# The first expert block's rows picked by TensorE inside the router phase, and block 1 of the second stage turned inside block 0's products

## The chip, the cores and the metric

The kernel runs on one core of one Trainium2 chip, as one launch. It computes two transformer blocks one after the other on 512 tokens of width 1024, all in float32. The metric is the device time of one execution in microseconds (us). Each core has a matrix engine (TensorE, PE below), a vector engine (DVE), a scalar engine (ACT), GpSimd (POOL) and SyncE (SP), which here only issues DMAs. Matrix products land in eight PSUM banks of 128 x 512 float32 words.

## The reference, cut to what matters

Both blocks end in a mixture of experts (MoE). Block 1 has 32 experts of width 256 and picks 2 of them per token; block 2 has 32 experts of width 1024 and picks 4. The second block's MoE is the same in outline, with a bias, a clamp and another gate.

```python
h2 = modulate(rms_norm(x, norm_ffn[l]), shift2, scale2)
ffn = hierarchical_moe(h2, ...)

def hierarchical_moe(h, w_group, b_group, w_router, b_router, w_gate, w_up, w_down):
    t = h.reshape(-1, d)                       # 512 x 1024
    ...                                        # softmax over groups, then top 2 of the experts of one group
    combine = ...                              # 512 x 32, two weights per token
    for e in range(N_EXPERTS):
        hid = jax.nn.silu(t @ w_gate[e]) * (t @ w_up[e])
        out = out + combine[:, e:e + 1] * (hid @ w_down[e])
```

The kernel computes for each expert only the tokens that chose it.

## The kernel before, in words

`two_blocks` calls a chain of phases. Each phase is a set of instruction streams, one per engine, and ends in a barrier of all engines. The change touches two phases, and each runs twice (names with rt1 and ex1 for the first MoE, rt2 and ex2 for the second; "first stage" and "second stage" below).

**The router phase** (`router_phase`, lines 1642 to 1872). The activations stand in `xT`, features on partitions. PE turns them (`turn_rows(n)`, line 1700: four 128x128 transposes each, n from 0 to 7, two per 128 tokens), ACT scales them by each token's inverse norm into `htok(i)` (line 1740; tokens 0 to 255 into the two slots of `x_rows`, the rest into `rt_late`) and stores them to DRAM as `rows` (line 1743). Meanwhile DVE picks the experts of each token; `asg` is the 0-1 matrix of tokens by experts. PE counts the tokens of each expert (lines 1708, 1710), ranks each token inside its expert (`lt` and `pre`, lines 1712 and 1717), and spreads a table of constants to all partitions (`beats`, `chosen`, lines 1715 and 1719). From these DVE works out (lines 1817 to 1841) the slot of each token in a list of rows. Then comes "the map": DVE and POOL make 0-1 matrices (`hot`, `put`) and PE multiplies them (line 1729), which turns "token to slot" into "slot to token". DVE and ACT write it out as `index` and `table` (lines 1859 to 1866). Between, PE runs products with no use (`keep_warm`, line 371). SP waits until the stores of `rows` have landed; then the phase ends.

**The expert phase** (`expert_phase`, lines 1886 to 2515). The experts are worked off in a fixed order of blocks, each with parts N (64 rows), Q (32 rows) or W (128 rows). In the first stage block 0 is one N part of 64 rows. In the second stage it is N and Q, 96 rows in all. For a block: POOL gathers its rows from `rows` by an indirect DMA with `index` (line 1880; `gather`), PE turns them (`transpose_x`, line 2112; eight tiles' worth, one call is `x_block`), ACT and in part DVE copy them from PSUM to `ex_xt` with the norm's gain and the modulation's shift (`copy_x`, lines 2266 and 2440), PE multiplies by the expert's up weights (`up_products`, line 2138), DVE and ACT apply the gate, PE turns the result (line 2156) and multiplies by the down weights (line 2179), DVE copies it out (line 2421) and ACT stores it.

PE works in this order: x_block(0), up(0), x_block(1), up(1), x_block(2), then the a and down steps of block 0, and so on. `ahead(b)` says for which blocks x_block(b + 1) is put between the products of up(b): before, only for some later blocks of the first stage.

The weights come in pieces of 1 MB. An expert's up weights are 2 pieces in the first stage and 8 in the second, its down weights 1 and 4. Sixteen places ("seats") hold them: `ring`, `x_spare` and `hT`. The first sixteen pieces are loaded before or during the router phase. Every later piece is issued by SP when PE has done the last product with the piece that sat there (line 2053, semaphore `used`). So the stream of weights starts again only when PE uses the first piece of block 0. `turns` (line 1955) loads a loop count from `table` into a register of each engine, at the start of the phase.

```python
x_block(0)
up_block(0)
x_block(1)
up_block(1)
```

## Time and profile before

| | us |
|---|---|
| median of 3 runs | 2619.21 |
| lowest, highest | 2614.50, 2623.94 |
| the profiled execution | 2614.59 |
| its span in the trace | 2612.8 |
| PE busy | 2383.2 (91%) |
| DVE busy | 1054.8 (40%) |
| ACT busy | 587.6 (22%) |
| POOL busy | 259.1 (10%) |
| HBM read | 640.14 MB |

All rows come from the profiled execution. Its own time lies 0.1 us above the lowest run and 4.6 us under the median. Times in the rows are microseconds from the start of the span. A row of the timeline is a run of equal instructions: start, length, engine, line, output and input, shapes, count, and in brackets how long the engine had stood idle before and what released it. A float32 product is two passes of PE, so that it counts twice in the trace; a transpose is one pass.
### The profile page before, as it was taken

The numbers are of one execution on the slowest core, as the hardware profiler recorded it, in microseconds if no ns is written. First come the engines' busy times: TensorE is split into PE (matmuls) and PEld (weight loads), VectorE is DVE, ScalarE is ACT, GpSimd is POOL, SyncE is SP. The second block draws the span as 40 slices with busy tenths as digits, with TensorE's granted clock in tenths as the row PEclk, the third lists the DMA queues.
The fourth block names the chain that finished last, engine by engine and source line by source line (L and its number), as shares of the span: only waits on it lengthen the run. The fifth ranks groups of instructions, "written<-read, shape, count | busy, mean of one in ns | idle before, by whom it ended". The sixth has DMA issues, their size and how long they took to land. (4 is left out here: it accounts for less than half of the span.)

```text
span 2612.8 us, 34138 instructions
## 1 busy us (share of the span) xinstructions
PE 2383.2 (91%) x12722; PEld 1153.3 (44%) x12722; DVE 1054.8 (40%) x2414; ACT 587.6 (22%) x1536; POOL 259.1 (10%) x272
## 2 busy tenths in 40 slices
PE   7999888989876999999999988999899998999984
PEld 3444666555344555667444442333233342333323
DVE  4856665743223655468332142232222322122215
ACT  3223532023222311364110011111111111111213
POOL 0000002111111000077200010000000000000002
PEclk8999978989988999899999989999999999999996
DMA  8533503979998310010314148999999999999995
GB/s 338 221 145 123 184 1 119 392 268 417 399 372 311 117 36 0 33 65 34 133 65 163 64 176 312 419 417 417 419 414 386 417 419 419 419 418 418 419 415 181
DMA packets 144204, 684.85 MB, mean 262 GB/s; under 512 B 16456, under 2 KB 44248, under 8 KB 78488
## 3 DMA queue, kind: packets, MB, share of 16 engines
q1 hardware_dynamic: 120920, 635.19, 60.3%
q0 software_dynamic: 9376, 25.19, 2.6%
q10 hardware_dynamic: 13744, 22.30, 2.3%
q8 instruction: 102, 1.67, 0.3%
q14 instruction: 62, 0.51, 0.1%
HBM read 640.14 MB, written 49.02 MB: 264 GB/s over the span
## 5 line engine op out<-in xcount | busy, mean ns | idle before, releaser
L2138 PE MATMUL bank<-ring,ex_xt 128*64 128x512 f32 (+4 forms) x2240 | 360.1, 507 | 24.4 <-DMA ring<-in_up 19.0
L2266 ACT ACTIVATE ex_xt<-bank,mod,gain 128x64 f32<-128x64 f32 (+2 forms) x472 | 151.0, 416 | 736.1 <-PE bank L2112 729.0
L2138 PE MATMUL bank<-x_spare,ex_xt 128*64 128x512 f32 (+4 forms) x1504 | 274.2, 522 | 23.5 <-DMA x_spare<-in_up 18.8
L2138 PEld LDWEIGHTS bank<-ring,ex_xt 128*64 128x64 f32 (+2 forms) x2240 | 125.3, 130 | 240.1 <-issue 194.3
L2179 PE MATMUL bank<-ring,ex_at 128*32 128x256 f32 (+2 forms) x1168 | 193.2, 502 | 13.8 <-DMA ring<-in_down 9.1
L1880 POOL DMA_INDIRECT x_rows<-rows,index x74 | 75.5, 1020 | 1078.5 <-PE bank L2112 1058.3
L2138 PEld LDWEIGHTS bank<-x_spare,ex_xt 128*64 128x64 f32 (+2 forms) x1504 | 98.1, 137 | 184.5 <-issue 147.0
L2179 PE MATMUL bank<-x_spare,ex_at 128*64 128x512 f32 (+2 forms) x720 | 133.8, 516 | 13.0 <-DMA x_spare<-in_down 12.1
L2680 PE MATMUL bank<-hT,ring 128*128 128x512 f32 x320 | 140.8, 594 | 2.5 <-ACT hT L2730 2.5
L2421 DVE COPY ex_y<-bank 128x512 f32<-128x512 f32 (+1 forms) x83 | 48.1, 599 | 214.6 <-PE bank L2179 214.5
L2179 PEld LDWEIGHTS bank<-ring,ex_at 128*32 128x32 f32 (+2 forms) x1168 | 61.1, 127 | 129.3 <-issue 109.0
L2378 DVE TENSOR_TENSOR ex_hb<-bank,ex_bias 128x512 f32<-128x512 f32 x40 | 27.5, 687 | 223.2 <-PE bank L2138 223.2
L1566 PE MATMUL bank<-u_mix,ring 128*128 128x512 f32 x256 | 114.2, 603 | 1.8 <-PEq L319 1.8
L2378 DVE TENSOR_TENSOR ex_hb<-bank,cst 128x512 f32<-128x512 f32 x40 | 27.5, 687 | 212.8 <-PE bank L2138 212.6
L633 PE MATMUL bank<-hT,ring 128*128 128x512 f32 x256 | 113.4, 597 | 0.0
L2680 PEld LDWEIGHTS bank<-hT,ring 128*128 128x128 f32 x320 | 60.4, 190 | 72.0 <-issue 70.2
L2179 PEld LDWEIGHTS bank<-x_spare,ex_at 128*64 128x64 f32 (+2 forms) x720 | 46.3, 134 | 89.3 <-issue 68.8
L3154 PE MATMUL bank<-hT,ring 128*128 128x512 f32 x192 | 83.8, 593 | 0.0
L2138 PE MATMUL bank<-hT,ex_xt 128*64 128x512 f32 (+4 forms) x400 | 78.6, 548 | 4.6 <-DMA hT<-in_up 4.6
L2278 ACT ACTIVATE ex_at<-bank 128x512 f32<-128x512 f32 (+2 forms) x62 | 28.4, 483 | 234.9 <-PE bank L2156 234.9
L633 PEld LDWEIGHTS bank<-hT,ring 128*128 128x128 f32 x256 | 48.0, 191 | 61.3 <-issue 61.0
L1566 PEld LDWEIGHTS bank<-u_mix,ring 128*128 128x128 f32 x256 | 48.4, 192 | 60.3 <-issue 60.2
(583 smaller groups left out, 3336.3 us busy)
## 6 DMA issues: line engine op xcount, KB each, us to landing
ring<-in_up SPq DMA_DIRECT2D x170, 1024.0 KB, 23.3
x_spare<-in_up SPq DMA_DIRECT2D x120, 1024.0 KB, 26.0
ring<-in_down SPq DMA_DIRECT2D x82, 1024.0 KB, 26.7
x_spare<-in_down SPq DMA_DIRECT2D x64, 1024.0 KB, 22.1
hT<-in_up SPq DMA_DIRECT2D x30, 1024.0 KB, 19.0
ring<-in_w_in SPq DMA_DIRECT2D x14, 2048.0 KB, 12.8
ring<-in_w_ada SPq DMA_DIRECT2D x12, 2048.0 KB, 8.4
ring<-in_w_mod SPq DMA_DIRECT2D x12, 2048.0 KB, 8.8
```

Of the source, the lines that this page charges most:

```text
L633: last = nc.tensor.matmul(o[:, :], w[:, kk, c0:c0 + P], k.hT[:, kk, :], **f)
L1566: last = nc.tensor.matmul(k.ps[m][:, :], w[:, kk, m * P:(m + 1) * P], mix[:, h * KT + kk, :], start=h == 0 and kk == 0, stop=h == halves - ...
L1880: pool.indirect_dma_start(out=to(p)[:, 0:D // groups], out_offset=None, in_=k.a["rows"].rearrange("r (g d) -> (r g) d", g=groups), in_offs ...
L2138: last = nc.tensor.matmul(k.ps[up_bank(b, p, r)][g * rows:(g + 1) * rows, 0:c.stop - c.start], rows_in, w[:, c], start=kk == 0, stop=kk == ...
L2179: last = nc.tensor.matmul(out, rows_in, w[:, g * width:(g + 1) * width], start=f == 0, stop=f == FT - 1)
L2266: last = act.activation(to, of, ACT.Identity, scale=gain(kk), bias=shift(kk))
L2278: last = act.activation(space("at", parts, p, at)[:, at_:at_ + min(512, w)], k.ps[a_bank(b, p, at_ // P)][:, 0:min(512, w)], ACT.Copy)
L2378: dve.tensor_tensor(h, k.ps[bank][:, :], bias_rows, ALU.add).then_inc(s["h_free"], 1)
L2421: last = dve.tensor_copy(out[:, g * 512:g * 512 + w], k.ps[y_bank(b, p, g)][:, 0:w])
L2680: last = nc.tensor.matmul(bank(kind, m)[:, 0:n], w[:, kk, c0:c0 + P], src[:, kk, :], start=kk == 0, stop=kk == KT - 1)
L3154: last = nc.tensor.matmul(k.ps[m % 2][:, :], w[:, kk, (m % 4) * P:(m % 4 + 1) * P], k.hT[:, kk, :], start=kk == 0, stop=kk == KT - 1)
```

## The change

In both router phases the rows of block 0 are no longer gathered, but picked. Experts are taken in an order in which block 0 is always expert 0 (`plan.fixed`), so a token's rank inside expert 0 is its row in block 0. DVE works out `sel` (rank + 1 where the token chose expert 0, else 0). POOL makes from it `pick`, a 128 x 64 (first stage) or 128 x 96 (second stage) 0-1 matrix for each of the four groups of 128 tokens. PE multiplies `htok(i)` by it: 8 products for each of the four groups, 32 in all, summed into banks 2 and 3. ACT copies the result, with gain and shift, into `x_rows` slot 0, which is from then on the `ex_xt` of block 0. ACT waits for this until all stores of `rows` have landed, since slot 0 is the source of one of them.

For that, PE's order in the router phase is changed: the transposes come earlier, the product with `pre` comes right behind the one with `lt`, and the four useless products ahead of the map are gone. In the expert phase block 0 has no gather, no transposes and no copies; the two useless products at its start are gone. POOL gathers block 1, then waits for the end of up(0), clears slot 0 and gathers block 2. In the second stage `ahead(0)` holds: x_block(1) stands between the products of up(0), ahead of the sixth of eight.

```diff
-                for n in range(5):
+                for n in range(6):
                     turn_rows(n)
...
                 nc.tensor.matmul(k.ps[1][:, 0:NT * E], k.c("lt"), fl(asg), start=True, stop=False)
-                turn_rows(5)
+                pe.wait_ge(s["pre"], 1)
+                nc.tensor.matmul(k.ps[1][:, 0:NT * E], k.c("ones"), fl(pre), start=False, stop=True).then_inc(s["rank"], 1)
+                turn_rows(6)
                 pe.wait_ge(s["beats"], 1)
                 nc.tensor.matmul(k.ps[5][0:E, 0:E], k.c("ones", 0, E)[0:E, :], beats[:], start=True, stop=True).then_inc(s["order"], 1)
-                pe.wait_ge(s["pre"], 1)
-                nc.tensor.matmul(k.ps[1][:, 0:NT * E], k.c("ones"), fl(pre), start=False, stop=True).then_inc(s["rank"], 1)
+                turn_rows(7)
                 pe.wait_ge(s["chosen"], 1)
                 nc.tensor.matmul(k.ps[0][:, 0:PARAMS * E], ...).then_inc(s["params"], 1)
-                turn_rows(6)
-                turn_rows(7)
-                k.keep_warm(4, 7)
+                pe.wait_ge(s["tsb"], 2 * NT)
+                def first_rows(i):
+                    pe.wait_ge(s["pick"], i + 1)
+                    for kk in range(KT):
+                        c = kk % per_bank * wide
+                        bank = 2 + kk // per_bank
+                        last = nc.tensor.matmul(k.ps[bank][:, c:c + wide], htok(i)[:, kk * P:(kk + 1) * P], pick[:, i, :], ...)
+                    if i == NT - 1:
+                        last.then_inc(s["first_mm"], 1)
+
+                for i in range(NT):
+                    first_rows(i)
...
                 act.activation(m[:], m[:], ACT.Exp).then_inc(s["exp"], 1)
+                act.wait_ge(s["sent"], 16 * NT)
+                act.wait_ge(s["first_mm"], 1)
+                for kk in range(KT):
+                    c = kk % per_bank * wide
+                    for p, part in enumerate(first):
+                        ...
+                        act.activation(x[:, 0, at_:at_ + rows], k.ps[2 + kk // per_bank][:, c:c + rows], ACT.Identity, scale=gain(kk), bias=shift(kk))
                 act.wait_ge(s["what"], 1)
...
+                dve.wait_ge(s["rank"], 1)
+                dve.scalar_tensor_tensor(sel[:], rank[:, :, 0], 1.0, asg[:, :, 0], ALU.add, ALU.mult).then_inc(s["sel"], 1)
                 dve.wait_ge(s["params"], 1)
...
+                pool.wait_ge(s["sel"], 1)
+                for i in range(NT):
+                    pool.tensor_scalar(pick[:, i, :], k.c("slot", 0, wide), 1.0, sel[:, i:i + 1], ALU.add, ALU.is_equal).then_inc(s["pick"], 1)
                 pool.wait_ge(s["split"], 1)
...
-    ahead = lambda b: bias is None and 4 <= b < B - 1 and b + 1 not in (plan.big, plan.big + 1)
+    ahead = lambda b: b == 0 and bias is not None or bias is None and 4 <= b < B - 1 and b + 1 not in (plan.big, plan.big + 1)
...
-                gather(0)
                 gather(1)
                 n = turns(pool)
-                for b in range(B):
+                pool.wait_ge(s["used"], plan.up_index(0) + U)
+                pool.memset(x[:, 0, :], 0.0).then_inc(s["slot_clear"], 1)
+                pool.wait_ge(s["slot_clear"], 1)
+                gather(2)
+                for b in range(1, B):
...
-                k.keep_warm(2, 0)
                 n = turns(pe)
...
-                        if kk == 2 and between is not None:
+                        if kk == (5 if b == 0 else 2) and between is not None:
                             between()
...
-                x_block(0)
                 up_block(0)
-                x_block(1)
+                if not ahead(0):
+                    x_block(1)
                 up_block(1)
```

On PE, in the router phase of the first stage and the start of its expert phase, before. `xT` rows are the transposes, `rt_hot,rt_put` is the map, `ring,ex_xt` are up products:

```order
486 L1700 MATMUL bank<-cst,xT 128x128 x20
487 L1708 MATMUL bank<-rt_asg,cst 128x32 x4
488 L1710 MATMUL bank<-cst,rt_asg 32x1 x4
489 L1712 MATMUL bank<-rt_asg,cst 128x128
490 L1700 MATMUL bank<-cst,xT 128x128 x4
491 L1715 MATMUL bank<-rt_beats,cst 32x32
492 L1717 MATMUL bank<-rt_pre,cst 128x128
493 L1719 MATMUL bank<-rt_chosen,cst 128x160
494 L1700 MATMUL bank<-cst,xT 128x128 x8
495 L371 MATMUL bank<-cst 128x512 x4
496 L1729 MATMUL bank<-rt_hot,rt_put 32x110 x32
497 L371 MATMUL bank<-cst 128x512 x3
```

And the same place now:

```order
486 L1704 MATMUL bank<-cst,xT 128x128 x24
487 L1712 MATMUL bank<-rt_asg,cst 128x32 x4
488 L1714 MATMUL bank<-cst,rt_asg 32x1 x4
489 L1716 MATMUL bank<-rt_asg,cst 128x128
490 L1718 MATMUL bank<-rt_pre,cst 128x128
491 L1704 MATMUL bank<-cst,xT 128x128 x4
492 L1721 MATMUL bank<-rt_beats,cst 32x32
493 L1704 MATMUL bank<-cst,xT 128x128 x4
494 L1724 MATMUL bank<-rt_chosen,cst 128x160
495 L1731 MATMUL bank<-rt_pick,x_rows 128x64 x16
496 L1731 MATMUL bank<-rt_pick,rt_late 128x64 x16
497 L1744 MATMUL bank<-rt_hot,rt_put 32x110 x32
```

The 32 picking products stand where four useless ones stood, and four transposes moved ahead of the product with `rt_chosen`.

On PE at the start of the second stage's expert phase, before (`64x512` is a part N of block 0, `32x512` its part Q):

```order
1071 L2112 MATMUL bank<-cst,x_rows 128x128 x6
1072 L2138 MATMUL bank<-ring,ex_xt 32x512 x4
1073 L2138 MATMUL bank<-ring,ex_xt 64x512 x8
...
1080 L2138 MATMUL bank<-ring,ex_xt 32x512 x4
1081 L2112 MATMUL bank<-cst,x_rows 128x128 x6
1082 L2138 MATMUL bank<-x_spare,ex_xt 32x512 x4
```

And now:

```order
1070 L2167 MATMUL bank<-ring,x_rows 32x512 x4
1071 L2167 MATMUL bank<-ring,x_rows 64x512 x8
...
1075 L2167 MATMUL bank<-ring,x_rows 64x512 x4
1076 L2141 MATMUL bank<-cst,x_rows 128x128 x6
1077 L2167 MATMUL bank<-ring,x_rows 64x512 x4
...
1080 L2167 MATMUL bank<-ring,x_rows 32x512 x4
1081 L2167 MATMUL bank<-x_spare,ex_xt 32x512 x4
```

The six transposes of block 0 are gone, and those of block 1 moved from behind up(0) into it.

On POOL, at the start of the first stage's expert phase, before and now:

```order
32 L1880 DMA x_rows<-rows,index 128x512 x2
33 L1955 TENSOR_LOAD table
34 L1955 ISA x2
35 L1880 DMA x_rows<-rows,index 128x512 x4
```

```order
33 L1909 DMA x_rows<-rows,index 128x512
34 L1984 TENSOR_LOAD table
35 L1984 ISA x2
36 L2116 MEMSET x_rows 128x1024
37 L1909 DMA x_rows<-rows,index 128x512 x4
```

One gather less, and a clearing of slot 0 ahead of the gather of block 2.

## Rows read from the trace of the kernel before

**Rows 1.** The page: busy share of the DMA engines in 40 slices, in tenths.

```profile
DMA  8533503979998310010314148999999999999995
```

**Rows 2.** Stretches of the second expert phase: length, busy per engine, PEclk, DMA share, GB/s.

```profile
1549.00:1555.00 6.00, 5.79 (x18) 1.45 (x20) 3.40 (x8) 0.16 (x1) 0.00 (x0) 0.51 0.17 45
...
1580.00:1585.00 5.00, 5.00 (x18) 1.24 (x12) 3.60 (x10) 1.82 (x4) 0.00 (x0) 0.50 0.02 7
1585.00:1590.00 5.00, 5.00 (x30) 1.19 (x29) 0.96 (x1) 0.00 (x0) 0.00 (x0) 0.94 0.69 233
1610.00:1615.00 5.00, 5.00 (x30) 1.31 (x26) 1.45 (x5) 0.42 (x1) 0.00 (x0) 0.71 0.17 30
1615.00:1950.00 335.00, 318.91 (x1606) 107.00 (x1605) 86.95 (x198) 50.39 (x152) 12.24 (x12) 0.99 1.01 415
1950.00:1975.00 25.00, 25.00 (x83) 8.82 (x83) 4.21 (x9) 1.93 (x6) 1.21 (x1) 1.00 0.85 331
1975.00:2545.00 570.00, 545.17 (x2824) 188.93 (x2822) 140.02 (x324) 89.27 (x275) 23.13 (x24) 0.99 1.01 418
```

**Rows 3.** The same view, the first expert phase.

```profile
571.00:700.00 129.00, 116.90 (x1039) 60.85 (x1038) 41.22 (x143) 35.06 (x116) 18.95 (x19) 0.97 1.01 410
```

**Rows 4.** Timeline of PE at the start of the first expert phase.

```profile
567.01 3.67 PE L2138 MATMUL bank<-ring,ex_xt 128*64 128x256 f32 x32 [1.38 <-ACT ex_xt L2266]
```

**Rows 5.** Timeline of PE at the start of the second expert phase.

```profile
1549.21 24.68 PE L2138 MATMUL bank<-ring,ex_xt 128*32 128x512 f32 x128 [2.57 <-ACT ex_xt L2266]
...
1579.43 19.50 PE L2138 MATMUL bank<-x_spare,ex_xt 128*32 128x512 f32 x96 [4.73 <-ACT ex_xt L2266]
```

**Rows 6.** Line 1955: PE's loop count is in its register (both stages).

```profile
L1955 PEldq SEQ_ASSERT  x2: 26/27/28, 561.9 to 1541.3; - x2
```

**Rows 7.** Stretches: the clock in the two router phases.

```profile
535.00:549.00 14.00, 12.68 (x57) 10.46 (x58) 8.22 (x49) 5.08 (x8) 0.00 (x0) 0.50 0.93 357
...
1516.00:1518.00 2.00, 1.77 (x10) 1.42 (x9) 1.78 (x11) 1.47 (x3) 0.00 (x0) 0.67 0.99 418
1518.00:1520.00 2.00, 1.73 (x15) 1.45 (x16) 1.59 (x6) 1.18 (x2) 0.00 (x0) 1.00 1.01 385
...
```

**Rows 8.** Stretches with nothing on PE but passes of 48 columns (line 2690).

```profile
1062.00:1066.00 4.00, 4.00 (x38) 4.00 (x37) 2.82 (x4) 0.72 (x1) 0.00 (x0) 1.00 0.00 0
1068.00:1076.00 8.00, 8.00 (x39) 8.00 (x39) 0.00 (x0) 0.00 (x0) 0.00 (x0) 0.50 0.00 0
```

**Rows 9.** Timelines: PE passes of 64 columns, and of 48 at the lower clock.

```profile
423.39 2.00 PE L1325 MATMUL bank<-s_r,ring 128*128 128x64 f32 x16 [0.92 <-DVE s_r L1252]
...
1069.50 7.03 PE L2690 MATMUL bank<-ring,x_spare 128*128 128x48 f32 x32
```

**Rows 10.** Timelines: row copy, map, its reading, index; second map, row copies.

```profile
549.04 0.69 ACT L1740 ACTIVATE rt_late<-bank,rt_rn 128x512 f32<-128x512 f32 x1 [0.17 <-PE bank L1700]
...
553.95 2.79 PE L1729 MATMUL bank<-rt_hot,rt_put 128*32 128x110 f32 x64 [0.28 <-DVE rt_put L1684]
...
557.63 0.27 DVE L1859 TENSOR_SCALAR rt_whose<-bank 128x110 f32<-128x110 f32 x1
...
559.40 0.85 ACT L1756 ACTIVATE index<-rt_what 32x5 int32<-32x5 f32 x4
...
1530.81 6.22 PE L1729 MATMUL bank<-rt_hot,rt_put 128*32 128x150 f32 x128 [0.96 <-DVE rt_put L1684]
...
1546.68 2.48 ACT L2266 ACTIVATE ex_xt<-bank,mod,gain 128x64 f32<-128x64 f32 x8 [6.83 <-PE bank L2112]
```

**Rows 11.** SP in the first router phase: its last issue, its wait after it.

```profile
537.13 0.97 SPq L1690 DMA_DIRECT2D hT<-in_up  x2
...
SPq L1686 <- DMA rows<-rt_late: 21.0, 1, 21.0
```

**Rows 12.** POOL: its small operations on line 1684, and its first gathers.

```profile
L1684 POOL TENSOR_SCALAR rt_put<-cst,rt_rest,rt_code x6: 512/558/562, 553.4 to 1531.8; 128x32 f32<-128x32 f32 x6
...
561.90 1.22 POOL L1880 DMA_INDIRECT x_rows<-rows,index  x1 [7.44 <-issue]
```

60 lines of the change are left out of this document (31 added, 29 removed).

## The prediction

> **What bounds the kernel now.** I read the DMA line of the page first. In the second expert phase, the last 15 slices of 40, the DMA engines are 90% busy or more [rows 1]. The stretches make this exact: from 1615 on the DMA share is 1.01, except for 25 us from 1950 at 0.85, up to 2545 [rows 2]. The first expert phase shows the same from 571 to 700 [rows 3]. In these stretches the stream of weights sets the time, and no faster step of PE can shorten it. But the stream can start sooner: a piece is only loaded when PE has used the one in its seat. In the stretches with a share of 0.02 (1580 to 1585) and 0.17 (1549 to 1555, 1610 to 1615) the DMA engines wait for PE [rows 2]. So what PE reaches earlier before 1615 moves the whole stream, and the end with it. That is the test for each term: does PE start or finish the first two blocks of a stage earlier?
>
> **The change, second stage.** PE's register with the loop count is ready at 1541.3 [rows 6]; up(0) begins at 1549.21, after gather, transposes and copies [rows 5]. Now nothing stands between, so up(0) can begin at about 1541.5: 7.7 us.
>
> Then x_block(1). Before, its transposes come behind up(0), which ends at 1573.89, and up(1) waits for the copies until 1579.43, 4.73 us of it idle [rows 5]. Now they stand ahead of the sixth of eight products' groups, some 13 us into up(0), and its gather was issued at the very start (the first gather's issue took 1.22 us [rows 12]; it is there by then). ACT needs 16 copies at 2.48 / 8 = 0.31, so 5.0 us [rows 10], and three eighths of up(0), 8 us, are left to hide them. So 4.7 us go; the transposes' own 0.8 us stay.
>
> The clock comes back too. After the idle time ahead of up(0), PE ran at 0.51 over 1549 to 1555; that is 5.8 us at half speed, worth 2.9. After the idle time ahead of up(1) it ran at 0.50 until 1585 and at 0.94 over the next 5, so 6.2 us from 1579.43, worth 3.1 [rows 2, 5]. With no such idle time the clock has no reason to fall: 6.0 us. Three useless products of 512 columns still stand between the map and the phase's end. Together 7.7 + 4.7 + 6.0 = 18.4 us.
>
> Against this stands the longer router phase. The picking is 32 products, 64 passes, with 128 columns of weights each. At the full clock the nearest rows are 4.00 / 38 = 0.105 us a pass for 48 columns [rows 8] and 2.00 / 16 = 0.125 for 64, its end included [rows 9]: 6.7 to 8.0 us. It can begin when the last rows are copied, about 1524.5, since the transposes come a little earlier, and ends at 1531.2 to 1532.5. The map started at 1530.81 and ran 6.22 us because it followed DVE [rows 10]. With its inputs ready, its 128 passes at 2.79 / 64 = 0.044 take 5.6 us, so it ends at up to 1538.1 against 1537.03: 1.1 us. The moved transposes hold the product with `chosen`, for which DVE's chain waits, by 0.5 to 1 us. These overlap; I take 1.3 us. ACT's 16 copies (5.0 us) end at about 1538, while it would wait for the map anyway; they cost nothing at the full clock. The useless products that went had no reader.
>
> POOL's four picks, at 0.51 to 0.56 us for 32 columns [rows 12], bounded by twice that for 96, give 2.1 to 4.5 us, well ahead of PE's need, since a group of 16 passes takes 1.7 us or more. They cost nothing, unless they hold up DVE. The Trainium skill, "SBUF — State Buffer", section "Who interferes with whom", says that a DVE instruction with two SBUF inputs and a GpSimd instruction that reads SBUF exclude each other. No row shows it for this place; by it DVE's chain could end up to the picks' time later, and the sum would be 2 us worse in each stage.
>
> Second stage: 18.4 - 1.3 = 17.1 us, if picking runs at the full clock.
>
> **The change, first stage.** up(0) begins at 567.01 [rows 4]; the register is ready at 561.9 [rows 6], so at most 4.9 us are won. ahead(0) does not hold here, so x_block(1) and up(1) follow as before and keep the lead. But two things push the router's end out. First, ACT must wait for the stores of the rows. SP's wait for them lasted 21.0 us after its last issue at 538.1, so to 559.1 [rows 11]; at this time weights share the queues. Then 8 copies, 2.5 us, then the index and table writes, 1.4 us: 563.0 instead of 560.25 [rows 10], 2.7 us later even if PE is fast. Second, the clock. In all of 535 to 549 it stood at 0.50 with PE 91% busy [rows 7]. The four useless products of 512 columns that stood ahead of the map are gone. And a stream of 48-column passes that began at the full clock fell to 0.50 and stayed there for 8 us with PE never idle [rows 8]. Picking with 64 columns is nearest to that row. At half clock a pass takes 7.03 / 32 = 0.22 us [rows 9], so 14.1 us. From about 548 (the last copy ended at 549.73 before, and its transposes come earlier) it ends at 562.1; the map adds 2.8 to 5.6 us and ends at 564.9 to 567.7, where before 556.74 would do and 557.63 was soon enough [rows 10]. That is 7.3 to 10.1 later; I take 8.5.
>
> So the first stage gives 4.9 - 2.7 = 2.2 at the full clock and 4.9 - 8.5 = -3.6 at half. POOL's gather of block 2 now stands behind up(0) and a clearing of 1024 columns. Before, it could be issued during block 0's copies. With its 1.22 us of issue [rows 12] and some 3 to 5 us of landing in company of weights it comes about when x_block(2) wants it, and may be 0 to 2 us late; 1.0. That leaves +1.2 or -4.6. I take -4.6, because both rows on the clock point to half: nothing in those 14 us raised it.
>
> In the second stage I take the full clock. There the same transposes brought it from 0.50 to 1.00 within four us (the stretch with 0.67 holds the rise [rows 7]), and 96 columns are denser than 64. The Trainium skill, "TensorE: Matmul & The Clock Gate", section "Part 4: PE-mode transpose", says that transposes do not count as busy for the gate. The rise at 1517 speaks against it; by that rule the second stage too would begin picking at half clock, which is rival A.
>
> **The sum.** 17.1 - 4.6 = 12.5 us off. The profiled execution took 2614.59, the median of the three runs is 2619.21. These lie 4.6 apart and the sum is made in the one; I set it against their middle, 2616.9, and get 2604.4. A measurement of this kernel can tell about 0.3% (7.9 us) from no change.
>
> **The rivals.**
>
> A. Picking at half clock in the second stage as well. 14.1 us from 1524.5 end at 1538.6, and the map, 5.6 us at the full clock and 11.2 at half, ends at 1544.2 to 1549.8 against 1537.03: 7.2 to 12.8 later, say 10 in place of 1.3. 8.7 less: 2613.1. For it: that phase too begins at 0.50, and a stretch with 0.67 stands in it [rows 7]. Against it: the wider passes.
>
> B. Full clock in the first stage too, as one row of products following another closely may allow. 5.8 more: 2598.6. For it: PE's work there is now packed more densely. Against it: rows 7 and 8.
>
> C. Slower. One mechanism, the half clock, at its dearest: picking and map at half in both stages, and still half when up(0) and up(1) run. First stage 4.9 - 10.1 - 1.0 = -6.2. Second stage 18.4 - 6.0 - 12.8 = -0.4. Together 6.6 us slower: 2623.5. It decides from the point at which picking plus map take over 20 us beyond what they replace in the two stages together. Against it: dense up products brought the clock back within 7 us in the second stage, 0.50 to 0.94 [rows 2].
>
> D. The lead is made but does not arrive: something that does not move with PE sets the stream, so that 7.7 + 4.7 are swallowed where the DMA share dips to 0.85 at 1950 [rows 2]. Then only a few us are left: about 2614. For it: this dip. Against it: even there the DMA engines wait for PE's use of pieces, which would all be earlier.
>
> **How the numbers follow.** The likeliest case (half, then full) has 0.47, B 0.24, A 0.13, D 0.09, C 0.07. Faster by over 0.3% (under 2611.4) are the first two and 0.06 of A and D, where their costs come out low: 0.77. Within 0.3% are the other 0.16 of A and D and 0.03 of C: 0.19. Slower (over 2627.1) is the rest of C, with a further step late behind it: 0.04. The range: the low end is B with the lowest run as base and no loss at block 2, 2594; the high end is A and D with the median as base, 2616. Outside it I leave C and a rest, under 0.2.
>
> **What would show it.** up(0) of the second stage begins within 3 us of 1543, x_block(1) stands inside it, and up(1) follows without a wait and at a clock of 1.00: each step worth 7.7, 4.7 and 6.0 less 1.3. In the first stage: the time from the first to the last picking pass (7 or 14 us) with the granted clock beside it, and ACT's copies waiting for the stores. DMA shares near 1.00 behind both, with starts as much earlier as up(1) is. Wrong it would be if the picking takes 14 us in both, if up(1) of the second stage still waits, or if the stretch from up(1) to the end is longer than before.

## The result, and the profile after

| us | before | changed |
|---|---|---|
| median | 2619.49 (6 runs) | 2597.72 (6 runs) |
| lowest, highest | 2611.35, 2623.94 | 2589.63, 2602.64 |
| the profiled execution | 2614.59 | 2589.63 |
| its span | 2612.8 | 2587.2 |

The ratio is 0.9923, with a 95% interval of 0.9905 to 0.9941: 20.2 us off, 15.5 to 24.9. The change makes the kernel faster by more than the 0.3% that a measurement can tell. The time forecast was 2604.4, its range 2594 to 2616.

The two profiled executions lie 25.6 us apart in span, more than the ratio says. So the first task is to see which part belongs to the change. Landmarks on PE's timeline of the kernel before: the first transposes of the two router phases (line 1700), the first transposes of the combine phase (line 2622), and x_block(2) of the second stage (line 2112).

```profile
535.10 1.30 PE L1700 MATMUL bank<-cst,xT 128*128 128x128 f32 x5 [1.04 <-PEq L319]
833.10 1.09 PE L2622 MATMUL bank<-cst,cb_acc 128*128 128x128 f32 x8 [0.66 <-DVE cb_acc L2594]
1514.12 1.94 PE L1700 MATMUL bank<-cst,xT 128*128 128x128 f32 x8 [0.78 <-PEq L319]
1604.30 0.66 PE L2112 MATMUL bank<-cst,x_rows 128*128 128x128 f32 x4
```

The same landmarks, and the rows between them, of the changed kernel (line 1731 is the picking, line 1744 the map, line 2167 the up products, line 2141 `x_block`):

```profile
531.44 5.33 PE L1704 MATMUL bank<-cst,xT 128*128 128x128 f32 x24 [1.04 <-PEq L319]
543.05 3.79 PE L1731 MATMUL bank<-rt_pick,x_rows 128*128 128x64 f32 x32 [0.18 <-ACT rt_late L1755]
546.67 3.74 PE L1731 MATMUL bank<-rt_pick,rt_late 128*128 128x64 f32 x32
550.34 2.29 PE L1744 MATMUL bank<-rt_hot,rt_put 128*32 128x110 f32 x64
561.16 6.24 PE L2167 MATMUL bank<-ring,x_rows 128*64 128x256 f32 x32 [5.76 <-PEq L319]
569.37 3.67 PE L2167 MATMUL bank<-ring,ex_xt 128*64 128x256 f32 x32 [1.38 <-ACT ex_xt L2294]
827.42 1.09 PE L2646 MATMUL bank<-cst,cb_acc 128*128 128x128 f32 x8 [0.50 <-DVE cb_acc L2618]
1506.07 1.06 PE L1704 MATMUL bank<-cst,xT 128*128 128x128 f32 x8 [0.78 <-PEq L319]
1516.47 6.49 PE L1731 MATMUL bank<-rt_pick,x_rows 128*128 128x96 f32 x32
1522.80 3.74 PE L1731 MATMUL bank<-rt_pick,rt_late 128*128 128x96 f32 x32
1535.19 13.81 PE L2167 MATMUL bank<-ring,x_rows 128*32 128x512 f32 x80 [1.64 <-PEq L319]
1548.93 0.87 PE L2141 MATMUL bank<-cst,x_rows 128*128 128x128 f32 x6
1557.92 16.50 PE L2167 MATMUL bank<-x_spare,ex_xt 128*32 128x512 f32 x96
1579.79 0.66 PE L2141 MATMUL bank<-cst,x_rows 128*128 128x128 f32 x4
```

Subtracting landmark from landmark gives the ledger of the 25.6 us:

| stretch | before | changed | difference |
|---|---|---|---|
| start to first router phase | 535.1 | 531.4 | -3.7 |
| first router phase to combine (first stage) | 298.0 | 296.0 | -2.0 |
| combine to second router phase | 681.0 | 678.6 | -2.4 |
| second router phase to x_block(2) | 90.2 | 73.7 | -16.5 |
| x_block(2) to the end of the span | 1008.5 | 1007.4 | -1.1 |

The first and third rows hold no changed instruction. Their 6.1 us are spread between executions. The change itself shows 2.0 us in the first stage and 16.5 in the second, which the rest of the stage keeps and adds 1.1 to. The 2.0 lie inside the spread of that stage, as the table below shows.

Stretches of the changed kernel (length, busy per engine, PEclk, DMA share, GB/s) show how this came about:

```profile
543.05:550.34 7.29, 7.29 (x64) 7.22 (x65) 6.22 (x27) 1.60 (x3) 1.77 (x4) 1.00 1.02 425
1516.50:1523.00 6.50, 6.50 (x35) 6.50 (x35) 5.54 (x22) 1.50 (x2) 1.15 (x2) 0.57 1.01 411
1523.00:1526.50 3.50, 3.50 (x36) 3.41 (x36) 3.33 (x16) 0.00 (x0) 2.05 (x4) 1.00 0.08 34
1535.00:1558.00 23.00, 22.81 (x138) 6.57 (x142) 9.05 (x17) 6.32 (x18) 2.13 (x2) 1.00 0.69 274
1558.00:1574.00 16.00, 16.00 (x100) 4.35 (x96) 6.41 (x15) 0.83 (x2) 4.21 (x4) 1.00 1.01 408
1590.00:1925.00 335.00, 319.00 (x1611) 106.35 (x1608) 87.44 (x199) 51.27 (x156) 12.93 (x13) 1.00 1.01 416
```

In the second stage up(0) and up(1) run at 1.00 from end to end, where [rows 2] has 0.51 and 0.50. up(1) has no bracket in its row: it waited for nothing, where [rows 5] shows 4.73. The DMA share from 1590 on is 1.01, as in [rows 2], so the same stream runs, only earlier. In the first stage the picks ran at 1.00 in this execution, and up(0) started with 5.76 us of idle time before it and took 6.24 us where [rows 4] has 3.67.

### The profile page after: what moved, and what is told of

The parts are those of the page before. It is cut to its first block and busy times, and to the rows that moved or that the text cites. A ratio compares the mean times of both kernels' runs of the same rounds, so it can differ in the third digit from the quotient of the medians.

```text
span 2587.2 us, 34332 instructions
## 1 busy us (share of the span) xinstructions
PE 2370.9 (92%) x12816; PEld 1159.1 (45%) x12816; DVE 1052.5 (41%) x2402; ACT 590.0 (23%) x1548; POOL 261.4 (10%) x279
## 5 line engine op out<-in xcount | busy, mean ns | idle before, releaser
L2167 PE MATMUL bank<-ring,ex_xt 128*64 128x512 f32 (+4 forms) x2080 | 334.7, 505 | 23.1 <-DMA ring<-in_up 21.6
L2167 PEld LDWEIGHTS bank<-ring,ex_xt 128*64 128x64 f32 (+2 forms) x2080 | 118.0, 132 | 220.2 <-issue 177.1
```

The source lines that it names most:

```text
L2167: last = nc.tensor.matmul(k.ps[up_bank(b, p, r)][g * rows:(g + 1) * rows, 0:c.stop - c.start], rows_in, w[:, c], start=kk == 0, stop=kk == ...
```

## The experiments

**Two theories.** Theory S says that nearly all of the gain is the second stage's and that the first gives about 2 us. My prediction's step said that the first stage loses 4.6, because the picks (the products with `pick`) run at half clock there. The first four kernels tell these apart, and price the two terms that I thought largest.

All distances below are worked out from PE's timelines, as in the ledger, in us from the router phase's own first transpose. So what happens ahead of a phase does not disturb them. "Combine" is the first transpose of the combine phase, "end" is PE's last product. A dash means that the stage gathers its block 0. e5 is left out, since its added products move every landmark.

| profiled execution | 1: picks (clock) | 1: up(0) | 1: x_block(2) | 1: combine | 2: picks | 2: up(0) | 2: x_block(2) | 2: end |
|---|---|---|---|---|---|---|---|---|
| before | - | 31.9 | 41.2 | 298.0 | - | 35.1 | 90.2 | 1091.5 |
| before again (e11) | - | 31.0 | 42.0 | 302.8 | - | 35.1 | 90.2 | 1091.7 |
| e1 only second | - | 31.2 | 42.2 | 304.6 | 10.5 | 29.2 | 73.8 | 1074.5 |
| e2 only first | 13.9 (0.50) | 32.9 | 43.8 | 301.6 | - | 35.7 | 89.7 | 1091.4 |
| changed | 7.4 (1.00) | 29.7 | 41.5 | 296.0 | 10.1 | 29.1 | 73.7 | 1074.0 |
| changed again (e10) | 13.9 (0.50) | 32.9 | 43.6 | 300.5 | 10.2 | 29.1 | 73.7 | 1074.1 |
| e3 block 1 behind | 7.4 (1.00) | 30.2 | 42.3 | 297.5 | 7.4 | 26.7 | 77.7 | 1078.4 |
| e4 own store | 13.9 (0.50) | 33.0 | 44.1 | 304.9 | 10.0 | 29.1 | 73.7 | 1074.5 |
| e6 wide ahead | 7.3 (1.00) | 29.8 | 41.0 | 296.2 | 7.3 | 27.2 | 71.8 | 1075.4 |
| e7 wide, own store | 7.3 (1.00) | 26.4 | 38.7 | 298.4 | 7.3 | 28.5 | 73.1 | 1074.7 |
| e8 and block 1 ahead | 7.3 (1.00) | 26.6 | 40.4 | 298.7 | 7.5 | 31.8 | 76.4 | 1078.2 |
| e9 first shortened | 7.3 (1.00) | 26.0 | 36.4 | 289.6 | 7.4 | 26.7 | 71.3 | 1071.6 |
| e12 the same again | 7.3 (1.00) | 30.7 | 41.7 | 294.9 | 7.4 | 26.7 | 71.3 | 1071.1 |

**e1, the second stage alone.** The two phases of the first stage are the functions of the kernel before:

```diff
-            router_phase(k, "rt1", t, 4 + E, TOP1, True, 1, PLAN1, seats, late, x, oh, g(1), ...)
-            expert_phase(k, "ex1", ...)
+            router_gathered(k, "rt1", t, 4 + E, TOP1, True, 1, PLAN1, seats, late, x, oh)
+            expert_gathered(k, "ex1", ...)
```

> The change in the second stage alone; the first stage's two phases are those of the kernel before (block 0 gathered). Theory S (what the two profiled executions show): the first stage gained 1.9 us (from its router's first transpose to the product behind its expert phase, 289.5 before and 287.6 after), the second 16.5 (to x_block(2), 90.2 and 73.7). Then this kernel is some 16.5 us under the kernel before, about 2603, and 2 us over the changed one. My prediction's step (first stage costs 4.6): this kernel is 4.6 us under the changed one, about 2593. Rival N: more than 18.4 of the 25.6 us between the two profiled executions belongs to the change, by way of the first stage: then this one is over 5 us slower than the changed one, 2603 or more.

Measured: median 2601.08, ratio 0.9935 (0.9908 to 0.9961), so 17.0 us off. The second stage shows the changed kernel's distances within 0.5 us. That is theory S. The 2593 that the prediction's step asked for lies just outside the interval (2594.3 to 2608.2). Rival N asked for 2603 or more, which the interval holds, so e1's times alone do not exclude it. e2 prices the first stage by itself.

**e2, the first stage alone.** The same edit with `rt2` and `ex2`.

> The change in the first stage alone; the second stage's two phases are those of the kernel before. Theory S: 2 us under the kernel before, about 2617.5, with the picking at the full clock (7.4 us). My prediction's step: picking at half the clock, 14.1 us, and 4.6 us over the kernel before, about 2624. In the trace: router's first transpose to first up product 31.9 us before, 29.8 by S, over 35 by the prediction's step. The second stage shows the waits of before again (2.6 us ahead of up(0), 4.7 ahead of up(1)).

Measured: median 2615.61 in 12 runs, ratio 0.9991 (0.9974 to 1.0009): no difference that shows, between 6.8 us gained and 2.4 lost. A loss of 4.6 is outside. But the clock was as I had predicted and not as theory S had it: the picks took 13.9 us. So the clock is not the same in each execution, and half clock costs less than I said. The changed kernel run again (e10) shows the same, on PE's timeline and in the stretch:

```profile
548.11 7.09 PE L1731 MATMUL bank<-rt_pick,x_rows 128*128 128x64 f32 x32
554.99 7.04 PE L1731 MATMUL bank<-rt_pick,rt_late 128*128 128x64 f32 x32
561.95 2.77 PE L1744 MATMUL bank<-rt_hot,rt_put 128*32 128x110 f32 x64
569.26 3.67 PE L2167 MATMUL bank<-ring,x_rows 128*64 128x256 f32 x32 [1.76 <-PEq L319]
579.97 0.66 PE L2141 MATMUL bank<-cst,x_rows 128*128 128x128 f32 x4 [1.39 <-DMA x_rows<-rows,index]
```

```profile
548.00:562.00 14.00, 14.00 (x69) 13.78 (x71) 9.12 (x43) 1.65 (x4) 1.88 (x4) 0.50 0.77 321
```

64 passes in 14 us, 0.22 each, is the price that I had taken. The last row of the timeline shows the other cost: x_block(2) waits 1.39 us for the gather of block 2.

**e3, block 1 of the second stage behind up(0) again:**

```diff
-    ahead = lambda b: b == 0 and bias is not None or bias is None and 4 <= b < B - 1 and ...
+    ahead = lambda b: bias is None and 4 <= b < B - 1 and ...
```

> The changed kernel, but x_block(1) of the second stage stands behind up(0) again. Prediction's terms: up(1) waits 4.7 us for ACT's 16 copies and then runs 6.2 us at half the clock, 3.1 us lost: 7.8 us over the changed kernel, about 2605.5; in the trace the distance from the router's first transpose to x_block(2) is 81.5 in place of 73.7. Rival H (the transfer sets the end anyway): the pieces for blocks 2 and later are asked for as up(0) uses its own, so only part of the 7.8 us arrives at the end: 2598 to 2602. Rival C: the clock does not fall behind a wait of 4.7 us: 4.7 us, 2602.5.

Measured: median 2600.34, ratio 0.9952 (0.9933 to 0.9972), 12.6 us off where the changed kernel has 20.2. The intervals overlap, so the trace has to decide. PE's timeline:

```profile
1538.34 21.96 PE L2167 MATMUL bank<-ring,x_rows 128*32 128x512 f32 x128 [1.65 <-PEq L319]
1565.83 18.17 PE L2167 MATMUL bank<-x_spare,ex_xt 128*32 128x512 f32 x96 [4.73 <-ACT ex_xt L2294]
1589.37 0.66 PE L2141 MATMUL bank<-cst,x_rows 128*128 128x128 f32 x4
```

From up(0) to x_block(2) it is 51.0 us here and 44.6 in the changed kernel, 6.4 more; to PE's last product 1051.7 and 1044.9, 6.8 more. So what is lost at x_block(2) arrives at the end, against rival H. The distances in the table are 77.7 and not 81.5 because this execution's second-stage picks found full clock (7.4 us) where the changed kernel's took 10.1, though the router phase is the same code: up(0) came 2.4 us sooner. That is why I count from up(0). The wait is the 4.73 of before to the digit. The clock fell too, against rival C, but came back sooner than I expected:

```profile
1565.80:1571.00 5.20, 5.17 (x20) 1.29 (x22) 3.20 (x10) 2.42 (x4) 0.00 (x0) 0.67 0.50 194
1571.00:1585.00 14.00, 14.00 (x88) 3.71 (x86) 1.43 (x1) 0.00 (x0) 0.00 (x0) 1.00 0.94 361
```

The mean of 0.67 means some 3.5 us of 5.2 at half, so 1.7 lost where I had 3.1. The same pieces took 19.50 us before, 18.17 here and 16.50 in the changed kernel.

**e4, ACT's copies wait for one store.** Slot 0 is the source of the first of the four stores only (SP still waits for all four):

```diff
-                        act.dma_start(k.a["rows"][i * P:(i + 1) * P, :], htok(i)).then_inc(s["sent"], 16)
+                        act.dma_start(k.a["rows"][i * P:(i + 1) * P, :], htok(i)).then_inc(s["sent" if i else "sent0"], 16)
...
-                act.wait_ge(s["sent"], 16 * NT)
+                act.wait_ge(s["sent0"], 16)
```

> The changed kernel, but ACT's copies of the picked rows into slot 0 wait for the one store that reads slot 0, not for all four. In the first stage they can start at 550.6 in place of 555.7. Theory W (the wait for the stores is on the path): index ends about 555.3 and SP's wait for the other stores about 555.7, so the phase ends near 556 in place of 559.4, 3.4 us sooner; the idle time ahead of up(0), 5.76, shrinks to about 2.4, the clock stays up, and up(0) takes 3.7 in place of 6.2 us: 6 us in all, about 2592. Rival G: block 1's gather cannot come earlier, so what up(0) wins is lost ahead of x_block(1): 0 to 1 us. Rival L: the stores land one after the other so late that slot 0's own is no sooner than the last: no change.

Measured: median 2600.43, ratio 0.9931 (0.9907 to 0.9955), no better than the changed kernel. It tells nothing of the stores, since its picks ran at half clock and ended when the stores had landed anyway. ACT's timeline names PE, not the DMA, as what released it:

```profile
562.16 2.47 ACT L1773 ACTIVATE x_rows<-bank,mod,gain 128x64 f32<-128x64 f32 x8 [12.08 <-PE bank L1732]
```

**e5, streams of narrow products.** By now the clock had been the crux three times, so I measured it alone. The added products are useless:

```diff
                 k.keep_warm(3, 5)
+                n = 64 if stage == 1 else 48
+                for _ in range(80):
+                    nc.tensor.matmul(k.ps[5][:, 0:n], k.c("ident"), k.cst[:, 0:n], start=True, stop=True)
...
+                pe.wait_ge(x_in[1], gathers(1))
+                cols = 64 if bias is None else 96
+                for _ in range(80):
+                    nc.tensor.matmul(k.ps[0][:, 0:cols], k.c("ident"), k.cst[:, 0:cols], start=True, stop=True)
                 up_block(0)
```

> A measurement of the clock under narrow products, put into the changed kernel; their output is used by nothing. First stage: 80 products of 64 columns (160 passes) behind the router's three wide ones, so begun at the full clock, and 80 more of 64 columns ahead of up(0), behind a wait for the gather of block 1. Second stage: 80 of 48 columns in the first place, 80 of 96 in the second. Theory K (width decides, and 64 columns keep the level that they find: the picks ran 7.4 us at 1.00 in two executions and 13.9 us at 0.50 in two others): first place 1.00 for the whole 18 us; second place 0.50 for the whole 35 us if the wait has let the clock fall; the 48 columns fall to 0.50 and stay, some 30 us; the 96 columns begin at 0.50 and rise to 1.00 within some 7 us. Rival U (any unbroken row of products raises the clock in time; the picks at half clock only ended too soon): all four end at 1.00. Rival R (chance): levels go up and down within a stream.

The four streams on PE's timeline (first stage, then second), and their stretches:

```profile
569.28 17.97 PE L1749 MATMUL bank<-cst 128*128 128x64 f32 x160
591.54 34.40 PE L2261 MATMUL bank<-cst 128*128 128x64 f32 x160 [4.29 <-DMA x_rows<-rows,index]
1597.92 29.03 PE L1749 MATMUL bank<-cst 128*128 128x48 f32 x160
1632.12 20.77 PE L2261 MATMUL bank<-cst 128*128 128x96 f32 x160 [5.17 <-DMA x_rows<-rows,index]
```

```profile
570.00:586.00 16.00, 16.00 (x146) 16.00 (x145) 0.00 (x0) 0.00 (x0) 0.00 (x0) 1.00 0.00 1
592.00:612.00 20.00, 20.00 (x96) 20.00 (x96) 0.00 (x0) 0.00 (x0) 0.00 (x0) 0.50 0.00 1
1598.50:1603.00 4.50, 4.50 (x43) 4.50 (x42) 0.00 (x0) 0.00 (x0) 0.00 (x0) 1.00 0.00 0
1605.00:1626.00 21.00, 21.00 (x100) 21.00 (x100) 0.00 (x0) 0.00 (x0) 0.00 (x0) 0.50 0.00 1
1632.20:1637.00 4.80, 4.80 (x23) 4.80 (x24) 4.01 (x11) 0.00 (x0) 0.00 (x0) 0.50 0.04 10
1638.00:1652.00 14.00, 14.00 (x128) 14.00 (x127) 0.00 (x0) 0.00 (x0) 0.00 (x0) 1.00 0.00 1
```

The one execution, with the streams in it, took 2708.40. All four came out as theory K said. PE was never idle in any of them. The first 64-column stream, begun at full clock, kept 1.00 to its end. The second, the same products behind 4.29 us of idle time, stayed at 0.50 for 34 us. The 48 columns, begun at 1.00, fell and stayed at 0.50. The 96 columns, begun at 0.50, rose. Rival U falls. Rival R has little left: each stream ran once, but the picks of all executions agree, 7.3 to 7.4 us or 13.9 and nothing between in the first stage. So for picks of 64 columns what counts here is the clock when the first one starts. This kernel's own picks found 0.50 in the first stage too (13.9 us) and 1.00 in the second (7.4 us).

**e6, three wide products ahead of the picks,** in both stages:

```diff
+                k.keep_warm(3, 5)
                 pe.wait_ge(s["tsb"], 2 * NT)
                 def first_rows(i):
```

> The changed kernel with three useless products of 512 columns ahead of the picks, in both stages. Theory K: they lift the clock, and the picks run at 1.00 in both stages, 7.4 us each, where the second stage took 10.1 at first half, then full. They cost 2.9 us at the full clock. First stage: the stores (end 24.3 us after the router's first transpose) still hold ACT, so the index ends as in the changed kernel, and up(0) begins at 29.7 to 30.5 whether the picks would have run at half clock or not (32.9 there). Second stage: up(0) at 27 to 29 in place of 29.1. Rival U: three products are too few, or the picks fall back: 13.9 us in the first stage, up(0) over 35.

Measured: one run, 2593.11. The picks ran at full clock in both stages, up(0) came at 29.8 and 27.2, both in the expected bands. In the second stage the 2 us won at up(0) stand at x_block(2) (71.8 for 73.7) but not at the end (1075.4 for 1074.0); where they went is open. Over all executions the first stage's picks were at full clock in two of six without the wide products (the changed kernel, e3; not e2, e4, e5, e10), and in five of five with them (e6 to e9, e12). The wide products themselves took 2.8 us where they found full clock and more where they did not (4.38 here in the first stage). In the second stage picks without wide products ahead found full clock in four executions (e3, e5, e9, e12; 7.4 us) and half in the other four (the changed kernel, e1, e4, e10; 10.1 to 10.5 us). ACT's copies in the first stage again wait for the stores, since the picks are done early:

```profile
556.10 2.48 ACT L1773 ACTIVATE x_rows<-bank,mod,gain 128x64 f32<-128x64 f32 x8 [10.75 <-DMA rows<-rt_late]
```

**e7, the wide products and the one store together,** both edits as above.

> The last one together with ACT waiting only for the store of slot 0's rows. By theory K and W: picks at the full clock in both stages; in the first stage they end at about 21.5 to 22 us after the first transpose (18.9 plus 2.9), map 24, copies 24.5, so little is left of the stores' wait and up(0) begins near 29. In all 2 us a stage under the changed kernel where its picks ran at half clock, nothing where they ran at full: 2594 to 2599, not to be told from the changed kernel in the median, but to be seen in the distance from first transpose to up(0). Rival: the useless products cost their 2.9 us in full in both stages: up(0) at 32 and 32, 2600 to 2604.

Now the wait for the stores can be seen by what happens without it: up(0) of the first stage at 26.4 where e6 has 29.8, 3.4 us sooner, the size that theory W of e4 gave. My own expectation for this run, near 29, was too late: the picks ended at 19.8 and not at 21.5 to 22. The rival had up(0) at 32 in both stages, for 2.9 us of wide products paid in full; measured are 26.4 and 28.5. (e8 shows the rival's 32 in its second stage.) Yet the median, 2592.26, with the ratio 0.9922 (0.9891 to 0.9953), does not differ from the changed kernel's. PE's timeline says where part of the lead goes:

```profile
559.92 5.30 PE L2169 MATMUL bank<-ring,x_rows 128*64 128x256 f32 x32 [2.16 <-issue]
572.25 0.66 PE L2143 MATMUL bank<-cst,x_rows 128*128 128x128 f32 x4 [1.38 <-DMA x_rows<-rows,index]
```

up(0) still ran in part at half clock (5.30 for 3.67), and x_block(2) waits for the gather of block 2, which stands behind up(0) and the clearing.

**e8, x_block(1) inside up(0) in the first stage too:** `ahead = lambda b: b == 0 or ...`.

> The last one, and x_block(1) stands inside up(0) in the first stage too. Then up(1) follows up(0) without its 1.4 us wait. Theory P (the first stage's end goes by the start of up(0), since the weights for block 2 and later are asked for as up(0) uses its pieces): up(1) begins 1.4 to 2 us sooner, the end of the stage does not move by more than 1. Rival Q (it goes by up(1)): 1.4 to 2 us sooner at the end as well. Rival G (block 1's gather has not landed 2.3 us into up(0)): PE waits inside up(0), and the pieces come later: 1 to 3 us worse.

Measured: 2595.78, ratio 0.9918 (0.9892 to 0.9944). up(1) came 1.1 us sooner than in e7 (32.5 after the first transpose, 33.6 there), but the next step waited for it:

```profile
567.97 3.67 PE L2169 MATMUL bank<-ring,ex_xt 128*64 128x256 f32 x32
575.87 1.12 PE L2143 MATMUL bank<-cst,x_rows 128*128 128x128 f32 x4 [4.23 <-DMA x_rows<-rows,index]
```

The wait grew from 1.38 to 4.23, and the combine phase came at 298.7 against 298.4. So the gather of block 2 is the next limit of the first stage. Rival G's wait inside up(0) did not occur. That the end goes by up(0), as theory P has it, is not shown by this, since the new wait explains it as well. The second stage has the code of e7, and yet its up(0) came at 31.8 where e7 has 28.5, and its end 3.4 us later. The wide products had found half clock:

```profile
1525.58 5.49 PE L371 MATMUL bank<-cst 128*128 128x512 f32 x6
```

So the wide products make the picks' clock safe, but in such an execution they cost more than they give: the changed kernel, without them, has 29.1.

**e9 and e12, three limits taken off in turn.** The changed kernel with the wide products in the first stage only, the one store, and:

```diff
-                pool.memset(x[:, 0, :], 0.0).then_inc(s["slot_clear"], 1)
-                pool.wait_ge(s["slot_clear"], 1)
                 gather(2)
...
                 up_block(1)
-                x_block(2)
-                a_block(0)
+                if bias is None:
+                    a_block(0)
+                    x_block(2)
+                else:
+                    x_block(2)
+                    a_block(0)
```

and the like for ACT's two steps.

> The changed kernel with four things more, all for the first stage: three useless products of 512 columns ahead of the picks (first stage only), ACT waits for the store of slot 0's rows alone (both stages), no clearing of slot 0 ahead of block 2's gather (the slot holds finite values), and x_block(2) behind the a step of block 0, on PE and ACT. Theory (a chain of three limits, taken off in turn: clock, stores, gather of block 2): picks at the full clock, up(0) 26.4 us after the router's first transpose, block 2's gather issued 1.3 us sooner after up(0), x_block(2) at about 37.5 to 38.5, down(0) at about 37 where it was 40.9 in the run before last. Against the changed kernel, 43.8 from the same point, 6 us. Rival F: the weights for the later blocks, not these steps, set the stage's end, so nothing of the 4 to 6 us is seen at the combine phase's first product (296 to 305 us after the first transpose in nine executions). The second stage as in the changed kernel: 73.7 and 1074. Time 2590 to 2596.

> The kernel of the run before last but two (first stage shortened in four places), once more, to tell its gain from chance: its profiled execution was the fastest of its five. Theory: the steps are in the code, so the first stage shows the same distances again within 1 us, counted from the router's first transpose: picks at 1.00 from 12.5 to 19.8, up(0) at 26.0, x_block(2) at 36.4, and the combine phase's first product under 295, where the changed kernel had 296.0 and 300.5. Median 2584 to 2592. Rival (chance): the combine phase's first product at 296 or later, median 2593 or more.

e9: median 2588.06, ratio 0.9899 (0.9883 to 0.9915); the changed kernel beside it 2596.71, ratio 0.9924 (0.9908 to 0.9940). e12: 2593.76, ratio 0.9907 (0.9893 to 0.9922). The ten runs of the two have the median 2591.6, the twelve of the changed kernel 2596.7. So this version has the lowest median of the study, some 5 us or 0.2% under the changed kernel and 0.7 us under e7; the intervals overlap. In e9 the first stage is the shortest of all (combine at 289.6), and rival F is wrong there: the lead arrives. PE's timeline of e9 (x_block(2) still waits 0.84 us for its gather):

```profile
540.04 2.84 PE L371 MATMUL bank<-cst 128*128 128x512 f32 x6
556.21 3.67 PE L2168 MATMUL bank<-ring,x_rows 128*64 128x256 f32 x32 [1.82 <-PEq L319]
566.63 0.66 PE L2142 MATMUL bank<-cst,x_rows 128*128 128x128 f32 x4 [0.84 <-DMA x_rows<-rows,index]
```

But my expectation that the distances would come again within 1 us failed. e12 has up(0) at 30.7, x_block(2) at 41.7 and the combine phase at 294.9, since the wide products themselves began at half clock:

```profile
549.26 5.40 PE L371 MATMUL bank<-cst 128*128 128x512 f32 x6
```

They lifted the clock for the picks (7.3 us) and paid 5.4 us instead of 2.8 for it. The median, 2593.76, fell where the rival (chance) had it, 2593 or more, while the combine phase, under 295, fell where the theory had it. So part of e9's lead over the changed kernel was the level that it found. The first stage of this version is the shortest in e9 and the second shortest, at 294.9, in e12.

Another part is not the first stage's at all. I expected the second stage as in the changed kernel, 73.7 and 1074, and both executions show 71.3 and 1071.1 to 1071.6. There the picks, with no wide products ahead of them, found full clock (7.4 us for 10.1). e3 and e5 found it too without the edits of e9, so the 2.4 to 3 us are the level that was found, as far as these executions show, and not a gain of the version.

**e10 and e11, the changed kernel and the one before again,** for the spread.

> The changed kernel once more, beside the last one on the same chip. Second stage: x_block(2) at 73.7, the end at 1074.0 to 1074.5, within 0.5 us, since 96-column picks lift the clock by themselves. First stage: picks take 7.4 us (clock found at 1.00) or 13.9 us (found at 0.50), either; up(0) at 29.7 to 30.2 or at 32.9 accordingly. Time 2597 to 2601.

> The kernel before once more, for the spread of its stages. Second stage: x_block(2) at 89.7 to 90.2 us after the router's first transpose, end at 1091.4 to 1091.6. First stage: up(0) at 31.2 to 31.9, combine phase 298 to 305. The spread between executions of one kernel (2605 to 2628 in 18 runs) should lie in front of the first router phase and between the two, 6 to 13 us, not in the second stage, under 1 us.

e10: median 2596.71, ratio 0.9924 (0.9908 to 0.9940), the first result over again. The second stage agrees with the first execution of the changed kernel within 0.1 us. e11: one run, 2621.53; x_block(2) at 90.2 and the end at 1091.7, within 0.1 us. The start of the first router phase lies between 530.2 and 538.3 in the executions of all kernels, the distance between the two router phases between 967.7 and 987.5 where no stream was added. The first stage of the kernel before has 298.0, 302.8 and 304.6 (e1). Most of the spread of the total is made in these places. The second stage adds to it only where picks or wide products found another level: 3.3 us at x_block(2) between e7 and e8, which have the same code there.

A good part of the first stage's spread in the unchanged kernel can be placed. The stretches from 175 to 205 us behind the first transpose, before and e11:

```profile
710.10:740.10 30.00, 25.99 (x231) 13.12 (x228) 8.59 (x30) 7.06 (x26) 3.99 (x4) 0.94 0.72 278
712.32:742.32 30.00, 24.01 (x232) 11.98 (x231) 8.93 (x29) 9.06 (x32) 3.99 (x4) 0.95 0.60 221
```

Here the DMA engines are not busy throughout. The share of 0.60 for 0.72 is 3.6 us more of them idle, and x_block(2) came 0.8 later, together 4.4 of the 4.8 us between the two. What makes this dip longer or shorter is open.

## Why the prediction was right, and where it was not

**The bound.** Right. The stream waits for PE's use of the first pieces; what the second stage won by x_block(2), 16.5 us, stood in full at the end (17.6 from the landmark to the end of the span). Rival D, a lead that does not arrive, is refuted by this and by e3 (6.4 us at x_block(2), 6.8 at the end). One execution does not fit, e6, where 2 us did not arrive. Rival C was not seen: up(0) and up(1) of the second stage ran at 1.00.

**The second stage: 17.1 forecast, 16.5 measured at x_block(2), 17.5 at PE's last product.** The terms:

- up(0) sooner by 7.7 less 1.3, 6.4: measured 6.0 (35.1 to 29.1). The picks began where I had them (10.4 us into the phase, 1524.5 by the clock of before) but found half clock, so they took 10.1 us and not 6.7 to 8.0. In e3 they found full clock, took 7.4, and up(0) came at 26.7. So rival A was half true: the level at the start was half, and the clock rose on the way. That my 6.4 lies so near to the 6.0 is luck. It was made for picks at full clock, and with full clock the term is 8.4 us (35.1 to 26.7), since the transposes are then done sooner too and the picks begin at 8.8. The stage as a whole gives 18.9 us at x_block(2) in e12 (90.2 to 71.3) where I had 17.1. Two misses, the level and the cost at the full level, made up for each other.
- The half clock inside up(0), 2.9: measured 24.68 against 21.96 us, 2.7.
- The wait ahead of up(1), 4.7: 4.73, exact.
- The half clock inside up(1), 3.1: 19.50 against 16.50 us, 3.0. In e3 it was 1.7, since the same wait was followed by a shorter stretch at half. This term depends on the execution.

**The first stage: 4.6 us lost by the forecast, no loss in the runs.** This is the step that failed, and it is nearly the whole of the gap: 12.5 us forecast, 20.2 measured, 7.7 between. By the medians of e1 and e2 alone the stages are worth 17.0 and 2.4 us, so the first accounts for 7.0 of it. The 2.4 are not clear of nothing (6.8 gained to 2.4 lost); that it is not a loss of 4.6 is. Two things were wrong in it.

*The clock.* I took the 48-column stream that fell from 1.00 to 0.50 [rows 8] as the nearest row for 64 columns, and made half clock the one case. e5 shows that a stream of 64 columns is another matter: it keeps what it finds. And "nothing in those 14 us raised it" [rows 7] was read from one execution. In e11, the same kernel again, the clock rises to 1.00 some 4 us into the same phase and is back at 0.50 after 9. So picks at half clock occur in some executions (four of six) and at full in the others. Neither my case nor rival B is the kernel; it is a mixture. B's time of 2598.6 lies next to the median by accident: its gain of 18.3 us was 1.9 too small and its base 2.6 too low. What decides the level is only described here, not explained. In the second stage the phase began at 0.50 in e5, e9 and e12, rose within 4 us, and the picks found 1.00; it began at 1.00 in the changed kernel, e1, e4 and e10, had fallen to 0.50 within 9 us, and the picks found 0.50. But e3 began at 1.00 and kept it.

*The price of half clock.* I had up(0) at 3.6 us later, and x_block(2) a further 1.0. With half clock up(0) comes at 32.9 to 33.0, against 31.0 to 31.9 before: 1.6 later in the mean. The picks start at 11.3 to 11.8 us (e2, e4, e10), not 13, as the transposes were moved ahead, and the map behind them took 2.8 to 3.2 us, not up to 5.6. x_block(2) is then 2.1 later in the mean (43.8 of three, 41.8 before), not 4.6. At the combine phase even that is gone: 300.5, 301.6 and 304.9 against 298.0, 302.8 and 304.6. With full clock it is 296.0 and 297.5, some 5 us sooner by means of 296.8 and 301.8, where I had 1.2. Three and two executions with a spread of 6.6 us in the unchanged stage don't carry these means far. Why a later x_block(2) is made good I have not settled.

**Smaller terms.** ACT's wait for the stores: forecast to 559.1 on the clock of before, so 24.0 us into the phase; measured 555.70, 24.3. The index was done 2.8 us later in the phase, forecast 2.7. The 5.76 us of idle time that this left ahead of up(0) dropped the clock there and cost 2.6 us (6.24 for 3.67). I had not priced that: the phase's end lay on the stores, and the three useless products end 5.76 us before up(0). The gather of block 2 was forecast 0 to 2 late: 1.4 to 1.8 us of waiting in e2, e4, e7 and e10, none in the first execution of the changed kernel, where it landed within 3.8 us of the start of its issue, against 5.2 in e7. Why it landed sooner there is open. POOL's four picks took 2.0 us in the first stage and 2.4 in the second, at or just under the low end of the forecast (2.1 to 4.5).

**The range** held the median. The base was 2616.9, 2.6 us under the later median of before, so with the better base the forecast would have been 2607.0 and the miss larger.

## What to carry to other kernels

Ask of a row of narrow products not only how wide they are but what level the clock has when they begin; where a kernel keeps what it finds, give both levels a chance instead of choosing one. Measure a stage from its own first instruction: here the total varies by 20 us between executions of one kernel, while the stage that holds most of the change repeated within about 0.1 us in two executions each of the kernel before and of the changed one. But look at more executions than two: with the same code in that stage e3, e7 and e8 show differences of 2.4 to 3.3 us, by the level of the clock that was found. And a step that is taken off a chain (gather, stores, transposes of the next block) brings forth the next wait at once, so the gain of each edit is to be read at the end of the stage and not at the step.

## What the runs showed of the hardware that was not expected

- In e5 a row of 64-column passes with PE never idle stayed at 0.50 for 34 us and, begun at 1.00, stayed at 1.00 for 18 us. A pass takes 0.215 us at the one and 0.112 at the other. The 48-column stream took 29.03 us and the 96-column one 20.77 for the same count of 160: the wider one was the faster, by its clock.
- Transposes alone were followed by a rise. In the first stage of the changed kernel PE had done nothing but transposes for 4 us when the clock rose (first row; the second starts behind the rise). The Trainium skill, "TensorE: Matmul & The Clock Gate", section "Part 4: PE-mode transpose", says that they do not count as busy in the same way; this trace speaks against it, in float32 transposes. It is not the whole story: in the second stage of the same execution the router phase began at 1.00 with the same transposes, PE 80% busy in the first 2 us, small products followed, and the clock was at 0.50 from 6 us on.

```profile
531.44:535.40 3.96, 3.96 (x17) 3.14 (x18) 2.69 (x18) 2.33 (x5) 0.00 (x0) 0.50 0.69 248
535.70:539.00 3.30, 2.43 (x25) 1.91 (x23) 2.55 (x16) 1.62 (x3) 0.00 (x0) 1.00 1.00 348
```

- POOL's picks hardly met DVE. They began 0.5 to 1.3 us ahead of DVE's chain in the router phase, so that only 0.9 us of them (first stage) and 1.1 (second) ran beside it in the first execution of the changed kernel. From its copy of the spread constants to the start of its last step ahead of `hot` the chain took 6.68 us before and 6.67 changed in the second stage, 6.00 and 6.13 in the first. The 0.13 are one instruction with two inputs in SBUF (`over`), which took 0.33 us beside a pick and 0.19 before. In the second stage of e3, where more of the picks fell beside DVE, they took 2.66 us in place of 2.41, and `over` 0.19. The Trainium skill, "SBUF — State Buffer", section "Who interferes with whom", would have the two engines exclude each other in such a place. The traces fit that at most in these small amounts, 0.14 us on DVE or 0.25 on POOL, and in e10 `over` took 0.19 beside a pick as well. The 2 us a stage that the prediction worked out from it did not come, and what a longer overlap would cost no run here shows.
